# A transformer block pair on one core: the first modulation in four chunks of 256 features instead of four of 512 of one kind

## What is computed

```python
def rmsnorm(x, g):
    xf = x.astype(jnp.float32)
    y = xf * lax.rsqrt(jnp.mean(xf * xf, axis=-1, keepdims=True) + EPS)
    return (y * g.astype(jnp.float32)).astype(x.dtype)

def modulate(h, shift, scale):
    return h * (1 + scale) + shift
...
sh1, sc1, g1, sh2, sc2, g2 = jnp.split(
    (jax.nn.silu(c) @ ada_w[layer] + ada_b[layer])[:, None, :], ADA_CHUNKS, axis=-1)
csh1, csc1, cg1, csh2, csc2, cg2 = jnp.split(
    jax.nn.silu(c_ctx) @ ada_w[layer] + ada_b[layer], ADA_CHUNKS, axis=-1)
h = modulate(rmsnorm(x, norm1_g[layer]), sh1, sc1)
hc = modulate(rmsnorm(ctx, norm1_g[layer]), csh1, csc1)
q, k, v, gu, gv, ga, gb = jnp.split(h @ w, IN_SPLITS, axis=-1)
```

## Time and profile before

| | |
|---|---|
| Median of 3 runs | 2413.39 us |
| Lowest and highest | 2410.26, 2413.77 us |
| Span of the profiled execution, first to last instruction | 2411.4 us |
| Granted TensorE clock, mean over the span | 0.998 |
| Busy share of the span: TensorE, VectorE, ScalarE, GpSimd | 98%, 65%, 39%, 52% |
| Memory traffic, mean | 218 GB/s |
| First q product; first k product | 27.84 us; 57.02 us |

### The profile page before, as it was taken

How to read it: one execution, slowest core, us unless ns; L and a number is a source line. 1 busy time by engine, 2 the same in 40 slices (tenths; PEclk the granted TensorE clock), 3 DMA queues, 4 the chain that set the end, 5 groups by cost and what they waited for, 6 DMA issues and landing times.

```text
span 2411.4 us, 35928 instructions
## 1 busy us (share of the span) xinstructions
PE 2367.4 (98%) x12892; PEld 2127.2 (88%) x12892; DVE 1567.8 (65%) x2831; ACT 945.5 (39%) x1488; POOL 1244.2 (52%) x704
## 2 busy tenths in 40 slices
PE   7999999999999999999999999999999999999998
PEld 4878887899999999999999999997777888888886
DVE  5258535689899999779999999892266225422201
ACT  4374333344455555333333333342353223332312
POOL 2305443337899999555555555444304444444443
PEclk9999999999999999999999999999999999999999
DMA  7227522327978898999999999943202222222231
GB/s 283 80 115 258 182 91 84 133 94 255 324 252 301 299 328 309 396 379 414 416 415 409 417 408 414 370 166 106 82 14 96 97 96 96 96 93 99 90 102 70
DMA packets 179613, 526.14 MB, mean 218 GB/s; under 512 B 18240, under 2 KB 70896, under 8 KB 178224
## 3 DMA queue, kind: packets, MB, share of 16 engines
q1 hardware_dynamic: 120928, 345.24, 39.7%
q0 software_dynamic: 43024, 159.14, 17.0%
q10 hardware_dynamic: 15552, 20.36, 2.4%
HBM read 474.93 MB, written 49.73 MB: 218 GB/s over the span
## 4 chain that ended last, share of the span: by engine, by line
PE 91%; DVE 3%; DMA 2%; issue 2%; POOL 1%; ACT 1%; SPq 0%; ACTq 0%; DVEq 0%; POOLq 0%
PE bank L1372 21%; PE bank L1374 21%; PE bank L1373 21%; PE pair L1373 6%; PE pair L1372 6%; PE pair L1374 6%; PE pair L1726 1%; POOL wlo L714 1%; DMA wraw<-in_w 1%; PE bank L1889 1%; PE pair L1513 1%; PE bank L1552 1%; PE bank L1539 1%; DMA act_dram<-actb 1%; PE pair L1664 1%
## 5 line engine op out<-in xcount | busy, mean ns | idle before, releaser
L714 POOL TENSOR_TENSOR wlo<-wraw,whi 128x1024 fp32r<-128x1024 f32 x303 | 740.4, 2446 | 761.1 <-ACT whi L856 760.2
L1372 PE MATMUL bank<-HH,whi 128*128 128x512 f32 (+1 forms) x2048 | 740.2, 361 | 9.5 <-DMA T<-in_keys 3.0
L1373 PE MATMUL bank<-HL,whi 128*128 128x512 f32 (+1 forms) x2048 | 735.8, 359 | 0.0
L1374 PE MATMUL bank<-HH,wlo 128*128 128x512 f32 (+1 forms) x2048 | 735.7, 359 | 0.0
L856 ACT ACTIVATE whi<-wraw 128x1024 fp32r<-128x1024 f32 x456 | 481.8, 1058 | 632.2 <-PE pair L1374 337.4
L1372 PEld LDWEIGHTS bank<-HH,whi 128*128 128x128 f32 x2048 | 385.0, 188 | 54.8 <-issue 5.7
L1374 PEld LDWEIGHTS bank<-HH,wlo 128*128 128x128 f32 x2048 | 384.5, 188 | 40.3
L1373 PEld LDWEIGHTS bank<-HL,whi 128*128 128x128 f32 x2048 | 385.0, 188 | 39.6 <-issue 0.5
L780 POOL DMA_INDIRECT VROW<-in_w,which x128 | 206.0, 1609 | 190.5 <-DVE YROW L2522 178.0
L2454 DVE TENSOR_TENSOR wlo<-wraw,whi 128x1024 fp32r<-128x1024 f32 x153 | 186.4, 1219 | 20.9 <-ACT whi L856 20.0
L773 POOL DMA_INDIRECT X<-in_u_rows,which x128 | 149.0, 1164 | 57.3 <-DVE dots L2296 32.6
(11 more groups left out here) (447 smaller groups left out, 3815.1 us busy)
## 6 DMA issues: line engine op xcount, KB each, us to landing
wraw<-in_w SPq DMA_DIRECT2D x456, 512.0 KB
gate_dram<-GS SPq DMA_DIRECT2D x24, 1024.0 KB
GJ<-gate_dram SPq DMA_DIRECT2D x32, 768.0 KB
act_dram<-actb ACTq DMA_DIRECT2D x108, 184.0 KB
AJ<-act_dram SPq DMA_DIRECT2D x108, 184.0 KB
adaw<-in_ada SPq DMA_DIRECT2D x32, 512.0 KB
ada<-in_ada SPq DMA_DIRECT2D x16, 512.0 KB, 14.2
NB<-in_nab POOLq DMA_DIRECT2D x4, 1024.0 KB
```

The source lines that it names most:

```text
L714: nc.gpsimd.tensor_tensor(wlo[:, slot, :, :].rearrange("p k c -> p (k c)"), wraw[:, slot, :, :].rearrange("p k c -> p (k c)"), whi[:, slot ...
L1372: pe.matmul(out_, ah, bh, start=first, stop=False, **kw)
L1373: pe.matmul(out_, ah, bl, start=False, stop=False, **kw)
L1374: return pe.matmul(out_, al, bh, start=False, stop=last, **kw)
```

## The change

The 2048 columns are cut otherwise: chunk c now holds 256 features of the shift and the same 256 of the scale, so one chunk is all that two blocks of 128 features need. The input `ada1` is laid out to match, with the same bytes. Four things follow from it. SyncE loads chunk 0, tiles 2 and 3, then chunks 1, 2 and 3. VectorE's `modulated` runs four times over two blocks instead of two times over four. ScalarE handles one chunk's rows and then two blocks of `HH`, four times, with tiles 2 and 3 split after the first pair. And TensorE does the ones product first, then chunk 0 with its turn and four filler products instead of seven, and begins the q products of blocks 0 and 1; chunks 1, 2 and 3 lie among the q products, each after tiles 0 and 1 of the pair before, with its turn after tile 2.

```diff
             load_chunk(0)
-            load_chunk(2)
-            load_chunk(1)
             for g in (2, 3):
                 load_w(g, g, peeled=True)
-            load_chunk(3)
+            for c in range(1, 4):
+                load_chunk(c)
...
             first_root()
-            ada_rows(0, 0)
-            ada_rows(1, 2)
-            norm_apply(S, None, HH, range(4))
+            ada_rows(0)
+            norm_apply(S, None, HH, range(2))
             for g in (2, 3):
                 ahead(g - 3, 0)
-            ada_rows(2, 1)
-            ada_rows(3, 3)
-            norm_apply(S, None, HH, range(4, KB))
+            for c in range(1, 4):
+                ada_rows(c)
+                norm_apply(S, None, HH, range(2 * c, 2 * c + 2))
...
             pe.wait_ge(silu_c, 1)
-            ada_half(0, 0)
             pe.wait_ge(const_in, CONST0)
             norm_sum(S, KB - 1)
-            ada_half(0, 1)
-            ada_half(2, 0)
-            ada_half(2, 1)
-            ada_turn(0, 0)
-            ada_turn(1, 2)
-            warm(7)
+            ada_chunk(0)
+            ada_turn(0)
+            warm(4)
             pe.wait_ge(w_lo, G0["q"] + 2)
             queries((0, 1), 0)
             ada_chunk(1)
             pe.wait_ge(w_lo, G0["q"] + 3)
             queries((2,), 0)
-            ada_turn(2, 1)
-            ada_chunk(3)
+            ada_turn(1)
             pe.wait_ge(w_lo, G0["q"] + 4)
-            queries((3,), 0, range(2))
-            ada_turn(3, 3)
-            queries((3,), 0, range(2, 4))
-            queries((0, 1), 1)
-            queries((2,), 1)
-            queries((3,), 1)
+            queries((3,), 0)
+            for c in (1, 2):
+                queries((0, 1), c)
+                ada_chunk(c + 1)
+                queries((2,), c)
+                ada_turn(c + 1)
+                queries((3,), c)
+            queries((0, 1), 3)
+            queries((2,), 3)
+            queries((3,), 3)
             norm_sum(CTX, 2 * KB - 2)
...
-            def modulated(h):
-
-                for kb in range(4 * h, 4 * h + 4):
+            def modulated(c):
+
+                for kb in (2 * c, 2 * c + 1):
                     nc.vector.tensor_tensor(T[:, kb, :], X[:, kb, :], bank[4][:, :], ALU.mult).then_inc(n_rows, 1)
-                v.wait_ge(ada_col, 2 * h + 2)
-                a, b = COLS["adab"][0], COLS["n1"][0] + 4 * h
+                v.wait_ge(ada_col, c + 1)
+                a, b = COLS["adab"][0], COLS["n1"][0] + 2 * c
...
-                for k in range(5):
-                    kb = 4 * h + k
-                    if k < 4:
+                for k in range(3):
+                    kb = 2 * c + k
+                    if k < 2:
```

More of the change, by code:

```diff
@@ L918, in _, with ada_rows @@
             norm_squares(X, S, [(0, x_in, 16), (4, const_in, CONST0)])
-            def ada_rows(turn, c):
-                act.wait_ge(ada_done, turn + 1)
-                nc.scalar.activation(mrow[:, c, :], bank[7 - c // 2 * 2][:, :], ACT.Copy).then_inc(ada_row, 1)
+            def ada_rows(c):
+                act.wait_ge(ada_done, c + 1)
+                nc.scalar.activation(mrow[:, c, :], bank[7 - c % 2 * 2][:, :], ACT.Copy).then_inc(ada_row, 1)
             for g in (0, 1):
@@ L1434, in ada_half @@
                         r = 64 * (p % 2) + 32 * j
-                        mm = pe.matmul(bank[7 - c // 2 * 2][r:r + 32, :], cpad[:, 2 * p + j, :],
+                        mm = pe.matmul(bank[7 - c % 2 * 2][r:r + 32, :], cpad[:, 2 * p + j, :],
                                        ada1[:, 4 * c + p, j * S:(j + 1) * S], start=(half == 0), stop=(half == 1))
@@ L1443, in ada_chunk, with ada_turn @@
                 ada_half(c, 1)
-            def ada_turn(turn, c):
-                pe.wait_ge(ada_row, turn + 1)
+            def ada_turn(c):
+                pe.wait_ge(ada_row, c + 1)
                 a0, a1 = COLS["pick"]
@@ L1458, in warm, with queries @@
                     pe.matmul(bank[2][:, :], whi[:, 0, 0, :], whi[:, 0, 0:4, :].rearrange("p k c -> p (k c)"), start=True, stop=True)
-            def queries(tiles, half, blocks=range(4)):
-                for kb in range(4 * half + blocks[0], 4 * half + blocks[-1] + 1):
+            def queries(tiles, c):
+                for kb in (2 * c, 2 * c + 1):
                     pe.wait_ge(n_lo, kb + 1)
@@ L1465, in queries @@
                                   kb == KB - 1) for u in tiles]
-                if half:
+                if c == 3:
                     for mm in done:
@@ L2089, in _ @@
             then(nc.vector.reciprocal(bank[4][:, :], bank[4][:, :]))
-            def modulated(h):
-                for kb in range(4 * h, 4 * h + 4):
+            def modulated(c):
+                for kb in (2 * c, 2 * c + 1):
                     nc.vector.tensor_tensor(T[:, kb, :], X[:, kb, :], bank[4][:, :], ALU.mult).then_inc(n_rows, 1)
-                v.wait_ge(ada_col, 2 * h + 2)
-                a, b = COLS["adab"][0], COLS["n1"][0] + 4 * h
+                v.wait_ge(ada_col, c + 1)
+                a, b = COLS["adab"][0], COLS["n1"][0] + 2 * c
                 then(nc.vector.tensor_tensor(
[L2098 to L2102, removed]
-                for k in range(5):
-                    kb = 4 * h + k
-                    if k < 4:
+                    mod[:, 0:16, :].rearrange("p (s c b) w -> p s c b w", s=2, c=4)[:, :, c],
+                    bank[6][:, 8 * c:8 * c + 8].rearrange("p (s b w) -> p s b w", s=2, b=2),
+                    bc(cols[:, a:a + 16].rearrange("p (s c b) -> p s c b", s=2, c=4)[:, :, c], 3, 2), ALU.add))
+                then(nc.vector.scalar_tensor_tensor(gsc[:, 0, 2 * c:2 * c + 2], mod[:, 8 + 2 * c:10 + 2 * c, 0], 1.0,
+                                                    cols[:, b:b + 2], ALU.add, ALU.mult))
+                for k in range(3):
+                    kb = 2 * c + k
+                    if k < 2:
                         v.wait_ge(n_rows, kb + 1)
@@ L2112, in modulated @@
                                                 ALU.subtract).then_inc(n_lo, 1)
-            modulated(0)
-            modulated(1)
+            for c in range(4):
+                modulated(c)
             scaled[2] += KB
@@ L2892, in pack @@
         ada=inp["ada_w"][0][:, 16 * P:].T.reshape(32, P, D),
-        ada1=inp["ada_w"][0][:, 0:16 * P].reshape(4, 2, P, 4, S).transpose(3, 0, 2, 1, 4).reshape(16, P, D),
+        ada1=inp["ada_w"][0][:, 0:16 * P].reshape(D, 2, 4, 2 * P).transpose(0, 2, 1, 3).reshape(4, 2, P, 4, S).transpose(3, 0, 2, 1, 4).reshape(16, P, D),
         cc=np.stack([inp["c"][0], inp["c_ctx"].reshape(D)]).reshape(2, KB, P).transpose(2, 1, 0),
```

## The result

The changed kernel takes 2416.97 us, the median of 21 runs (2415.35 to 2418.65). The kernel before takes 2412.78 in the runs beside it (21 runs, 2410.26 to 2415.51). The ratio is 1.0018, with a 95% interval of 1.0012 to 1.0025: slower by 0.12 to 0.25%, and within the 0.2% by its middle. The profiled execution has a span of 2415.0 us against 2411.4. The difference is 4.2 us in the medians, and 3.6 between the two profiles.

What follows compares the result with a forecast made beforehand. TensorE, busy 98% of the span, was taken as the bound. 2.5 us at the k tiles plus 0.9 for the clock made 3.4: span 2411.4 to 2414.8, median 2.0 higher, 2416.8; range 2411.5 to 2420.0, within 0.2%.

Steps and rivals of the forecast that it cites:

- The start: Up to the first q products: ones product ahead and smaller first chunk start them at 22.8 instead of 27.84, gain 5.0 us.
- bounded by the reciprocal chain: At the start: `mod` begins at 20.4, set by ones product, root, reciprocal and multiplications, with the modulation ready at 19.6 to 20.4.
- The weights and SP's queue: Tiles 2 and 3 and reordered loads add no wait; GpSimd's tiles are ready at 26.2 and 28.6, asked for about 27.6 and 30.0.
- The middle: Among q products: a third chunk costs 2.7 us; parts 9.64 apart against 8.6 of work, three waits of 1.0 to 1.1.
- rival (b): TensorE's waits in q and ahead of k don't appear, handoffs being shorter: k tiles 3.2 us earlier, 2410.2; 15%.
- What is late next: Between q and k: context squares, adds and emptying bank 0 leave TensorE idle 2 us; first k tile at 59.5, against 57.02.
- Rival (c): A second context add falls beside GpSimd's subtraction: +2.0 us, 2418.8; 5%.
- The clock: Around the first q products: granted clock falls again as before, now reaching products on the path; adds 0.9 us.
- I take the middle, 0.9: Price of the fall at the first q products: between nothing and 1.7 us, for a low stretch of 3.4 us.
- Rival (a): Low clock comes back at the three waits or the idle ahead of k: up to 1.7 us each, 2418.5 or 2420.2; 17%.
- The sum: Whole kernel: 2.5 us at the k tiles plus 0.9 for the clock, 3.4 us slower, 2416.8, 0.14%.
- the shift at the k tiles is found again at the end: Behind the first k tile: a shift of its start counts one to one in the end time; otherwise the whole prediction is wrong.

Runs made afterwards that it cites:

- experiment 1: Kernel before, with only the ones product put ahead of the first half chunk: 2414.51 us, ratio 1.0008.
- experiment 2: Changed kernel with the ones product back behind the first half chunk: 2421.31 us, ratio 1.0035 to the kernel before.
- Experiment 3: Changed kernel with chunks 2 and 3 computed at the end of the pair before, turns directly behind tiles 0 and 1: 2413.59 us, ratio 1.0004 to the kernel before.
- experiment 4: Changed kernel with the context's ones product behind k tile 0, which is written to bank 5: 2416.48 us, ratio 1.0014 to the kernel before.
- experiment 7: Changed kernel with GpSimd's subtraction for k tile 0 held back until VectorE has added the context's squares: one run, 2420.33 us.
- experiment 8: Changed kernel with Experiment 3, experiment 4 and experiment 5 together, q tile 0 finished before q tile 1, k tile split earlier: 2411.51 us, ratio 0.9994 to the kernel before.
- experiment 5: Changed kernel with eleven filler products instead of four: 2415.27 us, ratio 1.0015 to the kernel before.

## Why the prediction was right

**The start** was right in its cause. The step "bounded by the reciprocal chain" holds, and experiments 1 and 2 show that both halves of the change are needed for it. It was 0.5 too early, 22.8 for 23.28: the adds ended 0.2 later, since x landed 0.14 later in this execution and the adds then paused for 0.16, and the ones product took 2.04 where the earlier trace rows had 1.77.

**The weights and SP's queue** were no new wait, as said. GpSimd's subtractions of tiles 2 and 3 started at 23.95, against 23.9.

**The middle** was right to a tenth: pairs 9.65, 9.69 and 9.69 apart against 9.64, and three waits of 0.94 against 1.0 to 1.1. The last pair is 29.03 after the first products, against 28.9. Experiment 3 removed all three by order alone, so rival (b), that they don't appear, is out.

**What is late next** was right too: 7.75 from the last pair to the first k tile, against 7.8. The links are shown: the context's sum and the evacuation of bank 0, both together, by experiment 4, the add beside GpSimd by experiment 7 in one run. Rival (c), a second add in the collision, did not happen here, but it is what experiment 8 ran into when the subtractions began earlier: with four adds left, 8.0 us. Its price of 2.0 an add was right there: three adds of 2.43 instead of 0.43. The rule of the Trainium skill (GPSIMD Engine Reference, Specifications) on VectorE instructions with two SBUF inputs agrees with both experiments, 425 ns alone and up to 2432 beside GpSimd.

**The clock** was right as a tendency and wrong for the one profile of the changed kernel. "So I expect a fall here too": the profile after has none, 1.00 from 18 to 32, and four other executions with the same four fillers have it. Where it comes, its price was too small: "I take the middle, 0.9", and the runs show 1.6, 2.5, 2.1 and 2.5. The bound of 1.7 was read from a low stretch of 3.4 us in the earlier trace rows, while experiments 2 and 4 had low stretches that lasted longer: of the 12 first products nearly all stand 0.43 apart there, where the higher level has 0.23. Rival (a), a further fall at the waits of 0.94 or ahead of k, appears in no profile: the granted clock is 1.00 from 32 to 60 in all of them. But the prediction didn't look for falls further on, and the changed kernel's profile has both of its own there, at 428 and 1633.

**The sum.** Forecast 2.5 + 0.9 = 3.4; found 3.0 at the first k tile and 4.2 in the medians. The 2.5 is best seen between two executions without any fall before 2405, experiment 1 (which starts like the kernel before with its fillers at the high level) and experiment 5: 2409.6 and 2412.3, 2.7 apart. At the first k tile they are 3.6 apart (56.68 and 60.31, with x landing 0.2 later in experiment 5), and the wait of 0.85 that only experiment 1 has near 1016 gives most of the difference back. If the medians hold the same 2.7, some 1.5 of the 4.2 is left for the clock, an estimate, and it is the clock of the whole program: the mean granted clock of the changed kernel's 21 runs is 0.9968, against 0.9976 in the 27 runs of the kernel before beside experiments 1 to 4. So that term was too small, and the place given for it only one of three.

Two things in the agreement were luck. The forecast time of 2416.8 lies 0.2 from the median, but it stands on a median of three runs; on the 2412.78 of the runs beside the result, 3.4 more are 2416.2, 0.8 too low. And "the shift at the k tiles is found again at the end" holds as a number, 3.0 and 3.6, but not one to one: it was 2.0 at 1632, and the fall there brought it back. "Within" is what the ratio's middle says, with the upper end of its interval beyond the bound.

## What to carry to other kernels

Starting a dense stream earlier by cutting its input finer pays only if the later pieces arrive without a wait: count the whole handoff of one piece (here chunk, copy, turn, scale, split: 9.65 us against 8.6 of cover) and put each piece a stage ahead, which took all three waits away at no cost. Look also at what the old, longer tail was hiding; here a chain of 7 us for the context had 48 products over it and was left with 24. And when all waits that the profile names are gone, look at the neighbours: VectorE's adds, moved beside GpSimd's subtractions, gave part of the gain back here.

Before a difference of a few us between two profiles is put down to the change, look for low stretches of the clock in the whole of both. Here one weighs 1.6 us, and the effect 3 to 4.

## What the runs showed of the hardware

VectorE's add of two 128x256 tiles from SBUF takes 425 ns alone and up to 2437 beside GpSimd's subtraction, while its multiplication with one operand in PSUM is not slowed (in the kernel before, four take 2.48 alone, at 22.16, and 2.47 at 30.05, beside the subtraction from 30.43).

The granted clock can read 1.00 where the engine doesn't run at the higher level: the first half chunk took 1.94 us and a later one 1.06, with 1.00 shown for both stretches. The Trainium skill (TensorE: Matmul & The Clock Gate, Seeing it yourself) warns that clock events in a trace are not fully to be trusted; the durations of like instructions are the safer row.

Kernels whose starts are the same up to the first dense products (the changed kernel and experiments 3, 4 and 7) ran these at the higher level in one execution and at the lower level in three, where TensorE had done little ahead of them, and this was worth up to 2.5 us. Eleven unread products in the gap cost nothing, and in the three profiles that had them the clock stayed at the higher level. Seven did not help in the kernel before, where the fall came at 24.40, ahead of them.

Later in the program the clock falls at the same places in some executions and not in others, near 425 and 1630 us, and each fall is worth some 1.6 us.
